# Decode sums over cached rows: one 512-column product per sequence, or four 256-column products per pair of sequences

## What is computed

```python
def mem_attend(q, mem_kv):
    s = jnp.einsum('bthe,bmhe->bhtm', q, mem_kv[:, :, 0], preferred_element_type=jnp.float32)
    p = jax.nn.softmax(s, axis=-1)
    return jnp.einsum('bhtm,bmhe->bthe', p, mem_kv[:, :, 1].astype(jnp.float32)).astype(q.dtype)
...
    o = jnp.einsum('bhts,btshe->bthe', p / l, vg.astype(jnp.float32)).astype(q.dtype)
...
    mem_out = mem_attend(q, mem_kv).reshape(b, t, D_MEM) * jax.nn.silu(mg)
```

## Time and profile before

| | |
|---|---|
| median of 3 runs | 2760.17 us (2758.69 to 2760.25) |
| span of the profiled execution, first to last instruction | 2756.3 us |
| median over that span | 3.9 us |
| granted TensorE clock, mean over the span | 0.998 |
| TensorE busy | 2733.2 us, 99% |
| weight loads busy | 2260.7 us, 82% |
| VectorE, ScalarE, GpSimd busy | 1799.2, 1135.3, 365.7 us |
| the DMA engines' mean share on the hardware queue | 51.5% |

### The profile page before, as it was taken

How to read it: one execution, slowest core, us unless ns; L and a number is a source line. 1 busy time by engine, 2 the same in 40 slices (tenths; PEclk the granted TensorE clock), 3 DMA queues, 4 the chain that set the end, 5 groups by cost and what they waited for, 6 DMA issues and landing times.

```text
span 2756.3 us, 38909 instructions
## 1 busy us (share of the span) xinstructions
PE 2733.2 (99%) x13674; PEld 2260.7 (82%) x13674; DVE 1799.2 (65%) x3919; ACT 1135.3 (41%) x3409; POOL 365.7 (13%) x574
## 2 busy tenths in 40 slices
PE   9999999999999999999999999999999999999999
PEld 7788888888887788878887888788888889998787
DVE  7685766768688644335576667876674767777654
ACT  7532221312335234215434353532322359866532
POOL 0011010100101000000011032332423222210000
PEclk9999999999999999999999999999999999999999
DMA  8486545655676644324266676777777789657542
GB/s 280 146 255 208 186 146 193 191 190 157 219 245 198 190 125 149 97 100 147 99 246 227 221 254 231 255 271 269 238 253 265 259 317 322 228 191 247 192 141 90
DMA packets 291466, 567.59 MB, mean 206 GB/s; under 512 B 31568, under 2 KB 90512, under 8 KB 291272
## 3 DMA queue, kind: packets, MB, share of 16 engines
q1 hardware_dynamic: 257032, 462.31, 51.5%
q0 software_dynamic: 34240, 102.80, 10.4%
HBM read 432.28 MB, written 132.72 MB: 205 GB/s over the span
## 4 chain that ended last, share of the span: by engine, by line
PE 91%; DVE 5%; DMA 3%; ACT 1%; issue 1%; SPq 0%; POOL 0%; DVEq 0%; ACTq 0%; POOLq 0%
PE ps L129 25%; PE ps L131 25%; PE ps L130 25%; PE ps L4049 2%; PE ps L3652 2%; DMA tok_b_dram<-shared_o 1%; PE ps L4058 1%; PE ps L3690 1%; PE ps L3635 1%; PE ps L2387 1%; PE ps L2674 1%; PE ps L2958 1%; PE ps L2953 1%; PE ps L1378 1%; PE ps L1377 1%
## 5 line engine op out<-in xcount | busy, mean ns | idle before, releaser
L129 PE MATMUL ps<-b_wp,b_sring 128*128 128x512 f32 x640 | 249.7, 390 | 0.7 <-ACT ps L992 0.5
L131 PE MATMUL ps<-b_wp,b_sring 128*128 128x512 f32 x640 | 249.1, 389 | 0.0
L130 PE MATMUL ps<-b_wp,b_sring 128*128 128x512 f32 x640 | 249.0, 389 | 0.0
L129 PE MATMUL ps<-a_sring,a_wp 128*128 128x512 f32 x512 | 199.3, 389 | 0.0
L131 PE MATMUL ps<-a_sring,a_wp 128*128 128x512 f32 x512 | 199.3, 389 | 0.0
L130 PE MATMUL ps<-a_sring,a_wp 128*128 128x512 f32 x512 | 199.2, 389 | 0.0
L129 PE MATMUL ps<-b_wp,b_xthi 128*128 128x512 f32 x480 | 186.8, 389 | 0.1
L131 PE MATMUL ps<-b_wp,b_xtlo 128*128 128x512 f32 x480 | 186.8, 389 | 0.0
L130 PE MATMUL ps<-b_wp,b_xthi 128*128 128x512 f32 x480 | 186.7, 389 | 0.0
L992 ACT ACTIVATE ps<-shared_o 128x128 f32<-128x128 f32 (+1 forms) x408 | 108.1, 265 | 163.5 <-DVE shared_o L1169 143.5
L1169 DVE TENSOR_TENSOR shared_o<-ps,b_spare 128x512 f32<-128x512 f32 x160 | 109.6, 685 | 88.8 <-PE ps L131 78.2
(11 more groups left out here) (487 smaller groups left out, 6941.1 us busy)
## 6 DMA issues: line engine op xcount, KB each, us to landing
b_sring<-sums_dram SPq DMA_DIRECT2D x160, 512.0 KB, 5.1
a_sring<-sums_a_dram SPq DMA_DIRECT2D x128, 512.0 KB, 5.0
b_raws<-w_b_dram SPq DMA_DIRECT2D x176, 256.0 KB, 4.5
a_raws<-w_a_dram SPq DMA_DIRECT2D x140, 256.0 KB, 4.3
kv_dram<-shared_o POOLq DMA_DIRECT2D x96, 256.0 KB, 3.7
tok_b_dram<-shared_o POOLq DMA_DIRECT2D x96, 256.0 KB, 4.5
front<-tok_b_dram SPq DMA_DIRECT2D x96, 256.0 KB, 3.6
front<-grp_dram SPq DMA_DIRECT2D x48, 260.0 KB, 4.1
```

Source lines behind the costliest of these rows:

```text
L129: pe.matmul(acc, a_hi, b_hi, start=first, stop=False)
L130: pe.matmul(acc, a_hi, b_lo, start=False, stop=False)
L131: return pe.matmul(acc, a_lo, b_hi, start=False, stop=last)
```

## The change

Nothing is done at an even sequence any more, apart from its wait for `gated` or `sel_made`. At the odd one, both sequences of the pair are summed by four products of 256 columns: for each half of the 512 columns (`part`) and each of the two sequences (`odd`) one product, with its 8 output partitions beginning at partition 64 x part + 32 x odd of the same bank. So the even sequences' sums stand at partitions 0 (left half) and 64 (right half), the odd ones' at 32 and 96. The last of the four adds 2 to `gathered`. The four small products of the new token go to partitions 0 and 64, and now stand ahead of the whole pair.

`gate` becomes five VectorE instructions with waits on one another: the odd parts are copied from PSUM into `og`, 256 columns at a time; the even parts are added to them; and the sum is multiplied by the gate. Each adds 1 to `gated`; `GATES` is 5, and the waits for `gated` are rescaled: the first `mem` product waits until the four that read the bank are done.

```diff
+GATES = 5
...
+    def gathered_at(self, part, odd):
+
+        at = 2 * LOW * part + LOW * odd
+        return self.bank(slice(at, at + S), slice(part * C // 2, (part + 1) * C // 2))
...
-            pe.wait_ge(self.gated, 1)
+            pe.wait_ge(self.gated, GATES - 1)
+        if b % 2 == 0:
+            return
         pe.wait_ge(self.joined, self.joins_until(v))
         if kind == "dil" and b == S - 1:
             pe.wait_ge(self.nv_made, 3)
             for h in range(H):
-                pe.matmul(self.bank(slice(0, S), slice(h * HD, (h + 1) * HD)),
+                pe.matmul(self.gathered_at(h // 2, 0)[:, h % 2 * HD:(h % 2 + 1) * HD],
                           self.core.ident[0:self.HS, h * S:(h + 1) * S], self.nv[:, :], start=False, stop=False)
-        pe.matmul(self.bank(slice(0, S), slice(0, C)), self.sel[:, b * S:(b + 1) * S], slab[:, 0, :], start=(b == 0),
-                  stop=(b == S - 1)).then_inc(self.gathered, 1)
+        for part in range(2):
+            for odd in range(2):
+                n = b - 1 + odd
+                m = pe.matmul(self.gathered_at(part, odd), self.sel[:, n * S:(n + 1) * S],
+                              self.unit(v - 1 + odd)[2][:, 0, part * C // 2:(part + 1) * C // 2], start=(b == 1),
+                              stop=(b == S - 1))
+        m.then_inc(self.gathered, 2)
...
-        pe.wait_ge(self.gated, len(self.kinds))
+        pe.wait_ge(self.gated, GATES * len(self.kinds))
...
-        dve.tensor_tensor(self.og[kind].rearrange("s (h e) -> s h e", h=H),
-                          self.bank(slice(0, S), slice(0, C)).rearrange("s (h e) -> s h e", h=H), self.gates[kind],
-                          ALU.mult).then_inc(self.gated, 1)
+        at = GATES * (n - 1)
+        halves = [self.og[kind][:, part * C // 2:(part + 1) * C // 2] for part in range(2)]
+        for part, og in enumerate(halves):
+            dve.tensor_copy(og, self.gathered_at(part, 1)).then_inc(self.gated, 1)
+        for part, og in enumerate(halves):
+            dve.wait_ge(self.gated, at + part + 1)
+            dve.tensor_tensor(og, self.gathered_at(part, 0), og, ALU.add).then_inc(self.gated, 1)
+        dve.wait_ge(self.gated, at + 4)
+        og = self.og[kind].rearrange("s (h e) -> s h e", h=H)
+        dve.tensor_tensor(og, og, self.gates[kind], ALU.mult).then_inc(self.gated, 1)
```

## The result

The changed kernel takes 2744.71 us (median of 5 runs, 2743.17 to 2746.70), the kernel before 2760.05 (5 runs, 2758.69 to 2760.25): a ratio of 0.9946, 95% interval 0.9934 to 0.9957, 15.3 us less. The forecast was 2752.4 with a range from 2750.5 to 2763.6. The sign was right, the size half of what came, and the time lies outside the range, where the rival "all four groups at once" had put it (2744.6, chance 0.06).

What follows compares the result with a forecast made beforehand. TensorE's queue was taken as the bound where pairs stand; 7.74 us from the pairs plus 0.09 for the new token, minus 0, made 7.8 us less: span 2748.5, with 3.9 for the median 2752.4 us, range 2750.5 to 2763.6.

Steps and rivals of the forecast that it cites:

- all four groups at once: Rival for a pair's products on TensorE: all column groups run together, 15.6 us less, 2744.6 us; chance 0.06.
- What bounds the kernel: TensorE's queue is the path where the pairs stand; 12 pairs, 22.9 us in all, are what the change works on.
- Eight passes of 256 columns at 0.215: Pair's products on TensorE: eight passes of 0.215 us replace four of 512 columns; 1.72 us if one after the other.
- The two gaps of 0.09: TensorE before and after a pair: setting the array's shape waits until it is empty, 0.09 us each way; both stay.
- the slower rival: On TensorE, each new column group empties the array like a new shape: 3.1 us more, 2763.3 us; chance 0.13.
- Five slots: Pair on TensorE: a group's second pass overlaps the next group's first, 1.075 us; 0.645 less per pair, 7.74 in all.
- lower bound of 0.43: Pair's passes on TensorE with all four column groups together: 2 x 0.215 = 0.43 us, 1.29 less than now.
- Weight loads: Pair on TensorE: eight loads of 0.09 us hidden under passes, cost nothing; 3.2 us in all kept for the range.
- New token's products: Once, on TensorE: placed ahead of the whole pair, these small products leave one gap fewer, 0.09 us less.
- The gate: Three times on VectorE: five instructions take 1.48 us more, bounds 1.2 and 2.9; room of 1.0 us remains, cost nothing.
- What is late next: TensorE's wait for VectorE's combination after the transposes: a pair hides 1.75 us of slack, so the gain is kept.

Runs made afterwards that it cites:

- one group: Changed kernel, but a pair's four 256-column products all write partitions 0 to 7 and the gate is one instruction again; 2760.74 us beside 2759.31, ratio 1.0005.
- Heads by group: Against the kernel before: eight 128-column products per pair, one head per column group, each group's two products in a row; 2744.55 us beside 2759.31, ratio 0.9950.
- the uneven kernel: Changed kernel with its halves cut at column 384 instead of 256, giving passes of 384 and 128 columns; one time of 2745.25 us.
- The longer gate: Changed kernel with six more 8x256 copies in each of the three gates on VectorE; 2748.03 us beside 2759.86, ratio 0.9960.

## Why the prediction was wrong

**What bounds the kernel: right.** TensorE's queue was the path where the pairs stand; what the pairs lost, the time lost.

**Eight passes of 256 columns at 0.215: right** (0.216 with one group). The two gaps of 0.09 stayed as well: 0.32 after the last projection product, and 549 - 239 - 216 = 94 ns ahead of the transposes. That changing the group is no change of shape was right: groups follow one another after 7 ns, and the slower rival falls.

**Five slots: wrong, and this is the step that failed.** The prediction read from the earlier trace rows that TensorE starts instructions in the program's order, and took it to hold between groups. But every pass in those rows is in one group, where the order is kept; of passes of different groups they say nothing. The prediction says "if groups are independent" and yet lets the second pass of one group hold up the first of the next; groups that are wholly independent give two slots, its own lower bound of 0.43. That is what ran: first passes at 0, 6, 13 and 20 ns, second ones from 220. Heads by group show products, and the uneven kernel second passes, that start ahead of what stands before them in another group. The sentence ahead of the prediction that nothing moves an instruction ahead of another is thus true of the program's text and not of the starts on TensorE.

With two slots for five, 3 x 0.215 = 0.645 us more per pair are saved, 7.7 us in all, the size of the miss. The rival that had it was given 0.06, "against it: starts in order": one unproved reading was used twice, for the forecast and against the rival. The Trainium skill, "TensorE: Matmul & The Clock Gate", Part 3, states a strict order of starts and ends for packed products. The starts in the uneven kernel do not follow it; its increment, which lands after the end of the wide passes, does.

**Weight loads: right in the sum, with a price of nothing.** Eight loads begin within 28 ns and are done in 0.12 us, while passes over the same 128 rows are under way. The Trainium skill's rule in the same Part 3, that loads overlap products in flight only if the row group differs, does not hold for these four column groups over the same rows.

**New token's products: 0.09 for 0.52.** The saved gap was there, but the small products of heads 0 and 1 now run beside those of 2 and 3 as well: from 2572.11 to 2572.65 it is 0.54, where eight passes of 0.11 and a gap were 0.97. The same missed step.

**The gate: hidden, as said, but dearer.** 1.81 us more for 1.48: each copy and addition of 256 columns holds VectorE for about 0.45 up to the next, where the prediction took 0.34 for three of the four. The room ahead of the scores is 0.71 us and not 1.0. The longer gate shows that there is no more than that.

**What is late next: right.** In a step without a pair TensorE still waits for VectorE ahead of L3655 (1.08 us after the transposes begin), in steps with one it does not (0.93): 1.27 of 1.75 us are used up. ScalarE waits 4.5 us for slabs, for 2.4 before, but TensorE waits for nothing that follows from it, nor for `gated`.

**The range.** Its lower end, 2750.5, was drawn around five slots, with all that could be worse, and left out the one case that was better.

## What to carry to other kernels

A row that shows an order shows it for the units it contains: before an order is used to cap a gain, ask whether the rows hold two independent units at all. The plain float32 products of 8 output columns took two slots on four column groups where they took eight on one, and a pair of sequences was enough to fill them. Let the groups come in turn, or with at most two products in a row for one group: that took 0.55 to 0.58 us here, three in a row 0.91 and four 1.24. Give the work that puts the parts together to an engine that has room, measured against the next thing it delivers: the longer gate made the scores 2.05 us late and cost 3.7 with the granted clock of 0.50 that followed.

## What was not expected of the hardware

- Between column groups the starts leave the program's order: 128-column passes at 127 and 133 ns, ahead of 384-column passes of earlier products at 327 and 333. The increment on the last of them still lands at 876 ns, after the wide passes have ended.
- A group takes one running pass and three waiting, which is two products here; what stands behind that waits, for the other groups too (second group at 233 ns after eight passes in a row, at 122 after six, at 13 after four).
- Handing out costs 6.6 ns for each product of two passes. Four increments of the semaphore instead of one leave the pair on TensorE at 549 ns, but the last of them lands at 740 ns for 663.
